# Twelve tiles of the last gate's modulation, and not eight, are computed in the head of the feed-forward part

## The reference

```
mod = silu(c) @ w_mod + b_mod           # 6 vectors of 2048: shift, scale, gate for each half
h   = rmsnorm(x) * (1 + sc_a) + sh_a
z   = h @ w_in                          # 36 slabs of 128 columns: q, k, v of two head groups
o   = concat(diff_attention(z), banded_attention(z)) @ w_out
x   = x + gt_a * o
h2  = rmsnorm(x) * (1 + sc_f) + sh_f
u   = causal_conv3(h2 @ w_up)           # 2 * 5632 columns
x   = x + gt_f * ((silu(u_gate) * u_val) @ w_down)
y   = rmsnorm(x)
```

## Time and profile before

| | us |
|---|---|
| median of 3 runs | 2827.66 (2827.05 to 2828.97) |
| profiled execution, time | 2829.49 |
| profiled execution, span | 2827.7 |
| PE busy in the span | 2620.3 (93%) |
| PE weight loads busy | 2469.0 (87%) |
| DVE busy | 1658.2 (59%) |
| ACT busy | 994.1 (35%) |
| POOL busy | 638.3 (23%) |

### The profile page before, as it was taken

How to read it: one execution, slowest core, us unless ns; L and a number is a source line. 1 busy time by engine, 2 the same in 40 slices (tenths; PEclk the granted TensorE clock), 3 DMA queues, 4 the chain that set the end, 5 groups by cost and what they waited for, 6 DMA issues and landing times.

```text
span 2827.7 us, 50285 instructions
## 1 busy us (share of the span) xinstructions
PE 2620.3 (93%) x19815; PEld 2469.0 (87%) x19815; DVE 1658.2 (59%) x2930; ACT 994.1 (35%) x1975; POOL 638.3 (23%) x534
## 2 busy tenths in 40 slices
PE   6688888888999999789999999999999999999997
PEld 2267777777898899689999999999999999999997
DVE  6878777776445788785444444444444444444454
ACT  5555554554434433542222222222222222222224
POOL 4776566665100344331000000000000000000003
PEclk9889999999999999899999999999999999999998
DMA  9764444445221556253233333223333222322231
GB/s 299 229 196 147 157 137 155 148 146 144 61 63 47 154 165 174 74 157 110 83 89 90 91 90 90 87 80 90 90 90 91 86 83 87 91 85 84 87 105 67
DMA packets 416207, 325.00 MB, mean 115 GB/s; under 512 B 44394, under 2 KB 360202, under 8 KB 414880
## 3 DMA queue, kind: packets, MB, share of 16 engines
q1 hardware_dynamic: 410032, 302.55, 35.9%
q0 software_dynamic: 5248, 14.63, 1.6%
q10 hardware_dynamic: 688, 4.47, 0.4%
HBM read 307.73 MB, written 14.07 MB: 114 GB/s over the span
## 4 chain that ended last, share of the span: by engine, by line
PE 55%; DVE 5%; DMA 2%; issue 2%; ACT 1%; SPq 1%; ACTq 0%; POOL 0%; DVEq 0%
PE ps L1592 18%; PE ps L1590 18%; PE ps L1591 18%; DVE late_f L1279 3%; DMA w_raw<-in_w_out 2%; ACT w_hi L829 1%; SPq L538 1%; DVE w_lo L1188 0%; DVE x L1387 0%; DVE x_lo L1180 0%; ACT x_hi L1022 0%; DVE cv L1173 0%; PE ps L1809 0%; DVE late_f L1276 0%; DMA w_raw<-in_w_up 0%
## 5 line engine op out<-in xcount | busy, mean ns | idle before, releaser
L1590 PE MATMUL ps<-x_hi,w_hi 128*128 128x272 f32 x4480 | 1328.2, 296 | 44.7 <-DVE w_lo L1188 26.0
L1592 PE MATMUL ps<-x_hi,w_lo 128*128 128x272 f32 x4480 | 1308.2, 292 | 0.0
L1591 PE MATMUL ps<-x_lo,w_hi 128*128 128x272 f32 x4480 | 1298.0, 290 | 0.0
L1590 PEld LDWEIGHTS ps<-x_hi,w_hi 128*128 128x128 f32 x4480 | 855.1, 191 | 62.4 <-issue 23.8
L1591 PEld LDWEIGHTS ps<-x_lo,w_hi 128*128 128x128 f32 x4480 | 856.4, 191 | 0.0
L1592 PEld LDWEIGHTS ps<-x_hi,w_lo 128*128 128x128 f32 x4480 | 853.6, 191 | 0.0
L1188 DVE TENSOR_TENSOR w_lo<-w_raw,w_hi 128x1024 fp32r<-128x1024 f32 x432 | 536.5, 1270 | 463.8 <-ACT w_hi L829 462.7
L829 ACT ACTIVATE w_hi<-w_raw 128x1024 fp32r<-128x1024 f32 x432 | 442.0, 1056 | 837.2 <-PE ps L1592 545.3
L1591 PE MATMUL ps<-y_lo,w_hi 128*128 128x272 f32 x1408 | 407.3, 289 | 0.0
L1590 PE MATMUL ps<-y_hi,w_hi 128*128 128x272 f32 x1408 | 405.7, 288 | 0.0
L1592 PE MATMUL ps<-y_hi,w_lo 128*128 128x272 f32 x1408 | 405.0, 288 | 0.0
(11 more groups left out here) (200 smaller groups left out, 2221.8 us busy)
## 6 DMA issues: line engine op xcount, KB each, us to landing
w_raw<-in_w_mod SPq DMA_DIRECT2D x192, 512.0 KB, 4.7
w_raw<-in_w_up SPq DMA_DIRECT2D x176, 512.0 KB, 4.7
w_raw<-in_w_down SPq DMA_DIRECT2D x88, 512.0 KB, 4.4
w_raw<-in_w_in SPq DMA_DIRECT2D x56, 512.0 KB, 3.9
w_raw<-in_w_in SPq DMA_DIRECT2D x32, 256.0 KB, 3.7
w_raw<-in_w_out SPq DMA_DIRECT2D x16, 512.0 KB, 5.3
w_raw<-in_w_out SPq DMA_DIRECT2D x64, 128.0 KB, 3.9
x_transposed<-xT SPq DMA_DIRECT2D x4, 1088.0 KB, 5.7
```

The source lines that it names most:

```text
L1590: pe.matmul(out[:, 0:n], hi_w, hi_x, start=first, stop=False)
L1591: pe.matmul(out[:, 0:n], hi_w, lo_x, start=False, stop=False)
L1592: return pe.matmul(out[:, 0:n], lo_w, hi_x, start=False, stop=last)
```

## The change

One group moves from the mixer to the head. The mixer has nine groups, 72 chunks in the same 48 slots; the output projection has four as before, now groups 9 to 12; the head has three, groups 13 to 15, that is twelve tiles of the last gate, with three chunks at each of its eight places and not two. PE's sum of the head's first group stands ahead of tile 2, of the second ahead of tile 3 and of the third behind tile 3, in banks 4, 5 and 6.

```
-LATE1 = 10 * LPG
+LATE1 = 9 * LPG
 LATE2 = 4 * LPG
-LATE3 = 2 * LPG
+LATE3 = 3 * LPG
...
 for _j in range(GRP):
     for _q in range(2):
-        HEAD_LATE[_j, _q] = [LATE1 + LATE2 + 4 * _j + 2 * _q + _i for _i in range(2)]
+        HEAD_LATE[_j, _q] = [LATE1 + LATE2 + 6 * _j + 3 * _q + _i for _i in range(3)]
...
             for g in range((LATE1 + LATE2) // LPG, (LATE1 + LATE2 + LATE3) // LPG):
                 dve.wait_ge(m_late, LGT * (g + 1))
-                ins = late_cols(MOD_EARLY + LGT * g, LGT, bank(4 + g % 2))
+                ins = late_cols(MOD_EARLY + LGT * g, LGT, bank(4 + g - (LATE1 + LATE2) // LPG))
...
             for jj in range(1, GRP):
-                if jj == GRP - 1:
-                    late_tile((LATE1 + LATE2) // LPG, 0, LGT, bank(4))
+                if jj >= 2:
+                    late_tile((LATE1 + LATE2) // LPG + jj - 2, 0, LGT, bank(2 + jj))
                 up(jj, (4 * jj, None), 0)
                 up(jj, (4 * jj, None), 1)
-            late_tile((LATE1 + LATE2) // LPG + 1, 0, LGT, bank(5))
+            late_tile((LATE1 + LATE2) // LPG + 2, 0, LGT, bank(6))
```

## The result

The kernel after takes 2801.45 us in the median of four runs (2796.78 to 2803.14), the kernel before 2828.31 beside it. The ratio is 0.9895, with a 95% interval of 0.9879 to 0.9911: faster by 27 us, where 2842 us and a range from 2829 were forecast. The profiled execution took 2796.78 us, with a span of 2795.0 (32.7 less than before).

What follows compares the result with a forecast made beforehand. DVE was taken to set the pace in mixer and head, in the mixer also through late weight loads. Head 24.5 plus clock 3.5 minus mixer 14 gave +14 us: 2842 us, range 2829 to 2857, slower at 0.78.

Steps and rivals of the forecast that it cites:

- (c): Mixer: eight fewer late chunks and fewer tight weight loads (24 slots, not 32) give back 14 us, between 5.4 and 21.
- Faster. One mechanism: the tight wait: Rival, mixer: weight loads stop waiting for buffers just freed; 40 us gained, 12 us faster overall, 2816 us; chance 0.09.
- a mixer shorter by over 25 us: Sign of a wrong forecast: it would mean the tight loads were the mixer's pace, not the sums.
- ScalarE waits for w_in in odd slots only: Sign of a right forecast, mixer: ScalarE's waits for weight loads sit in odd slots only.
- PE waits newly for scores in slot 0 of a head: Sign of a right forecast, mixer: a new PE wait for scores in each head's slot 0.
- The lower bound of 0.7 us a chunk: Mixer: price of a removed chunk, from slots 51 to 53 without chunks; 5.4 us for eight.
- (a): Feed-forward head: eight added chunks lengthen DVE's cycle, 26.1 us, or 24.5 with a column sum hidden under a wait.
- (b): Head, tiles 2 and 3: longer PE waits lower the granted clock, costing 3.5 us of at most 5.
- (d): Output projection: places and counts stay, only group numbers shift; no change in time.
- Nothing back: Rival: weight loads stay late, so the mixer gives 0 to 3 us against the head's 28; 2853 to 2856 us; chance 0.10.
- balance: Rival: mixer gives the whole 21 us and the head's clock costs nothing, or some clock returns; 2829 to 2833 us; chance 0.13.
- the cheaper head: Rival, head: added instructions cost 0.75 us, not 1.65, 12 us, sum -2; its small chance is counted in that of balance.

Runs made afterwards that it cites:

- experiment 3: Kernel after with one late chunk in the even mixer slots and two in the odd ones, as many chunks and tight slots: 2804.73 us, ratio 0.9919.
- experiment 4: Kernel after (nine mixer groups) with the weight chunk loaded ahead of the late chunks in each mixer slot: 2780.64 us, ratio 0.9837.
- experiment 1: Kernel before (ten mixer groups) with the weight chunk loaded ahead of the late chunks in each mixer slot: 2782.38 us, ratio 0.9836.
- experiment 7: Kernel before with the weight chunk first in the mixer, and eleven groups in the mixer, one in the head: 2773.94 us, ratio 0.9799.
- the ninth: Kernel before with eleven groups in the mixer, four in the output projection, one in the head, weight chunks first in mixer and output projection: 2763.88 us, ratio 0.9763.
- Experiment 11: Kernel before with weight chunks first in mixer and output projection, single-chunk slots moved to places 3 and 5 of each head: 2771.2 us, ratio 0.9789.
- experiment 5: Kernel after with the load order changed so the 24 tight slots come in runs of two, same sums and places: 2834.18 us, ratio 1.0013.
- experiment 2: Kernel after with the weight chunk loaded behind all late chunks in each mixer slot, so every slot is tight: 2872.38 us, ratio 1.0162.

## Why the prediction was wrong

**The failed step is (c), the mixer.** It forecast 14 us, with 28 as the utmost; it was 59.4 (54.7 in slots 8 to 49). The rival "Faster. One mechanism: the tight wait" came nearest, priced at 40 us, and half of its mechanism is seen: the w_lo of slot 30 now starts 0.7 us behind the begin chunk of slot 29 (443.08 to 443.77), where it was 6.8. But the rival rested on an odd slot that does not slip, and it did: the w_lo of slot 29 starts 5.2 us behind its begin chunk (432.17 to 437.33), where it was 3.0. What the prediction gave as a sign, a mixer shorter by over 25 us, was seen. Its reading of that sign is half right: the order of loads accounts for 28.6 of the 54.7 us, the smaller count for 26.1. Two finer signs came as forecast and decided nothing: ScalarE waits for w_in in odd slots only, and PE waits newly for scores in slot 0 of a head (2.6 us in seven heads).

Inside the step, four things failed.

*The load was priced from one late row.* The prediction had w_lo of slot 29 wait for a load of 5.64 us and w_hi: 6.7 us from the end of the begin chunk. It took 5.2; before, the tight loads take 5.2 us in the mean from issue to w_lo, so the row of 6.7 was a late one. Then 7.1 us were forecast to the w_lo of slot 30, and 6.4 measured. So the lead at this place was 4.8 us and not 2.6.

*It was taken once a head.* There are two such places in a head, 1 and 4; they gave 4.4 and 3.8 us. The hand-written pair of slots began at a state copied from before, with the delay of the tight slots ahead of it already in its times. A late load has no single price: it is 1.6 us each in before, 0.7 or 1.2 where they stand alone.

*The chunk was priced where PE leads.* The lower bound of 0.7 us a chunk came from the empty slots 51 to 53. They take 26.9 us before and after, and PE is busy for 25.97 of them: what it shows there is the floor that PE sets, not what a chunk costs above it. Where DVE leads, a chunk took 4.0 us of DVE's busy time (27.9 us for seven), not the 2.2 of its two instructions at 1085 ns, since the instructions that stay became shorter as well. That depends on the placement: experiment 3, with nine groups too, is busy only 14.4 us less than before (2.1 a chunk).

*The clock was put at nothing.* PE's busy time fell by 19.1 us for the same products, at 0.99 for 0.95; the other 35.6 us of the 54.7 are time in which PE was not busy. No run changed the clock without the waits, so how much of the 19.1 would have come by itself stays open.

**Right in size: (a) and (b), the head.** 28 us were forecast, 28.3 measured; 35, 34 and 38 us for the tiles, and 34.9, 34.2 and 38.5 measured. The instructions cost 1.53 us each where 1.65 was taken (tiles 1 to 3: DVE busy +18.4 us, forecast 19.8), the first tile 7.0 us where 6.3 was taken. The first half tiles of tiles 1 to 3 took 23.5 us in all for 19.7: the 3.9 us stand for (b)'s 3.5, and the granted clock was 0.88, 0.90 and 0.87 in these tiles. The column sums went under a wait, as forecast. What (b) had wrong is the place of the waits: ahead of tiles 2 and 3 they were to grow to 6 or 7 us and are 0.35 and 0.18 beside the sum of 1.84, while 4.5 to 4.7 us stand inside each tile. PE's wait for w_lo reached 36.1 us and not 40 to 45: PE's busy time in the tiles grew by 10.1 us (one column sum more, the rest at the lower clock), and a slower PE fills part of the wait. The Trainium skill, "SBUF — State Buffer", section "Who interferes with whom", has a DVE instruction with two SBUF inputs and a reading GpSimd instruction exclude each other; an estimate by that rule, from the shortest instructions of before (0.74 and 1.34 us), is 2.1 us a pair. The trace does not agree with that sum: the stretches above stay at 1.53 us an instruction, although GpSimd runs eleven adds beside the twelve. How long an add excludes DVE, no run shows.

**Right: (d).** 240.3 and 238.8 us. Behind tile 3 the kernel kept its pace (+1.3). But the stage had 8 us in it: with its weight chunks first it took 232.6.

**Nothing back, balance, and the cheaper head** fall with the numbers above. With the weight first, balance is what the same change gives (experiment 4 against 1).

**Open.** Why the tenth group costs 26 us in the mixer and the eleventh 2 to 9 (2.2 by its stretch in experiment 7, 9.1 in the ninth). Experiment 11 excludes the places of the single slots. Between ten and nine groups DVE's busy time falls by 34.0 us for seven chunks (349.81 to 315.85), more than twice the chunks' own instructions: 15.5 us are these fourteen at 1104 ns, 11.1 the other 118 (1104 to 1010 ns each), 6.7 the 35 o_norm (968 to 779 ns). That they are shorter because GpSimd works beside them less often is argued only, since no run separated the two engines. Open too is why a late load costs less alone (experiment 5).

## What to carry to other kernels

Where one queue of loads goes round a ring of buffers, look up for each urgent load which item frees its buffer; a load that must wait for work just done belongs ahead of that work in the order, and here moving one line of the order was worth 46 us while the move of a whole group was worth 27. What a late load costs depends on what stands around it (0.7 to 1.2 us alone, 1.6 to 2.1 in rows or with nothing to do meanwhile), so a change of counts that shifts the late loads can act far beyond the work that it removes, and a hand-written stretch must begin in a slot whose own delay is recomputed. Price removed work in slots where the same engine leads, and before a price is taken as a lower bound ask which engine set the length there.

## What the runs showed of the hardware

Where PE waited less, its granted clock was higher: in slots 8 to 49 there were 13 stretches at the lower level before (granted clock 0.95), 3 after (0.99), 2 in experiment 4 (0.99), 7 in experiment 1 (0.97), 10 in experiment 5 (0.96), 13 in experiment 2 (0.94). Between before and after that is 19.1 us of PE's busy time, beside 35.6 us of time in which it was not busy. The same instruction of DVE took 1085 ns in the mean before and 1031 after in the mixer, and 1631 in the median in the head, where GpSimd's took 1591 beside it.
